# Two transformer blocks in one kernel on one core: order of work at the end of the second block's projections and at the start of its attention

## What is computed

```python
h = rms_norm(x, norm_g[l])
proj = h @ w_in[l]
cq, ckv, kr, dq, dk, dv, mq, z = jnp.split(proj, IN_OFFSETS_2, axis=-1)
y_mla  = mla_branch(cq, ckv, kr, ...)   # 8 heads; q from cq @ w_uq, k and v from ckv @ w_ukv, rms_norm per head, rope
y_diff = diff_branch(dq, dk, dv, ...)   # 4 heads with two maps each: p[0] - lam * p[1]
y_mem  = mem_branch(mq, mem, ...)       # 4 heads over 256 memory tokens
y = jnp.concatenate([y_mla, y_diff, y_mem], axis=-1) * jax.nn.silu(z)
x = x + y @ w_out[l]
```

## Time and profile before

| | |
|---|---|
| median of 3 runs | 1109.83 us (1109.31 to 1114.26) |
| the profiled execution | 1111.78 us, its span 1110.0 us |
| PE, busy | 1054.4 us (95%) |
| DVE, busy | 627.6 us (57%) |
| ACT, busy | 563.5 us (51%) |
| POOL, busy | 445.8 us (40%) |
| granted TensorE clock, mean | 0.982 |

### The profile page before, as it was taken

The page is one execution under the profiler, slowest core; times in us unless marked ns, Lnnn a source line. Parts: engine busy times, 40 slices in busy tenths (PEclk is TensorE's granted clock), DMA queues, the critical chain, the costliest instruction groups (busy, mean ns, idle before and its releaser), DMA issues.

```text
span 1110.0 us, 15249 instructions
## 1 busy us (share of the span) xinstructions
PE 1054.4 (95%) x5118; PEld 874.7 (79%) x5118; DVE 627.6 (57%) x1415; ACT 563.5 (51%) x1154; POOL 445.8 (40%) x215
## 2 busy tenths in 40 slices
PE   6999889999999999999999999999999989889798
PEld 4888778899888778888888888778887778666577
DVE  4536556888835466554545455442235988586732
ACT  5443667777724344444444444443244263887821
POOL 1444552343424443444444444414444244443323
PEclk9999999999999999999999999999999999898999
DMA  5364442111013332222223223243252122343213
GB/s 198 95 175 135 132 148 76 50 47 39 30 38 133 123 104 95 95 95 94 97 94 109 95 96 133 95 141 106 98 187 103 59 88 93 100 109 86 76 49 113
DMA packets 40604, 111.87 MB, mean 101 GB/s; under 512 B 7219, under 2 KB 10419, under 8 KB 39859
## 3 DMA queue, kind: packets, MB, share of 16 engines
q1 hardware_dynamic: 29724, 91.80, 25.3%
q10 hardware_dynamic: 10824, 19.35, 5.5%
HBM read 100.25 MB, written 7.96 MB: 97 GB/s over the span
## 4 chain that ended last, share of the span: by engine, by line
issue 44%; PE 26%; POOL 15%; DVE 8%; ACT 3%; DMA 1%; SPq 1%; POOLq 1%; ACTq 0%; DVEq 0%
POOL WLO L638 13%; PE PS L1816 6%; PE PS L1818 6%; PE PS L1817 6%; PE PS L1998 2%; PE PS L2021 2%; PE PS L1957 1%; PE PS L1958 1%; DVE PB L1326 1%; DMA X<-xT 1%; PE PS L2160 1%; ACT PB L879 1%; DVE BLO L1239 1%; DVE PB L1364 1%; ACT WHI L696 1%
## 5 line engine op out<-in xcount | busy, mean ns | idle before, releaser
L638 POOL TENSOR_TENSOR WLO<-RAW,WHI 128x1024 fp32r<-128x1024 f32 x155 | 376.4, 2429 | 542.7 <-ACT WHI L696 542.5
L696 ACT ACTIVATE WHI<-RAW 128x1024 fp32r<-128x1024 f32 x162 | 171.2, 1058 | 291.6 <-PE PS L1818 260.2
L1816 PE MATMUL PS<-HHI,WHI 128*128 128x512 f32 x648 | 257.4, 397 | 12.7 <-DVE HLO L1217 9.0
L1817 PE MATMUL PS<-HLO,WHI 128*128 128x512 f32 x648 | 255.0, 394 | 0.0
L1818 PE MATMUL PS<-HHI,WLO 128*128 128x512 f32 x648 | 254.6, 393 | 0.0
L1816 PEld LDWEIGHTS PS<-HHI,WHI 128*128 128x128 f32 x648 | 123.4, 190 | 41.1 <-issue 11.5
L1816 PE MATMUL PS<-BHI,WHI 128*128 128x512 f32 x368 | 145.2, 395 | 3.2 <-POOL WLO L638 1.8
L1818 PEld LDWEIGHTS PS<-HHI,WLO 128*128 128x128 f32 x648 | 123.4, 190 | 26.3
L1818 PE MATMUL PS<-BHI,WLO 128*128 128x512 f32 x368 | 143.4, 390 | 0.0
L1817 PE MATMUL PS<-BLO,WHI 128*128 128x512 f32 x368 | 143.3, 389 | 0.0
L1817 PEld LDWEIGHTS PS<-HLO,WHI 128*128 128x128 f32 x648 | 123.3, 190 | 25.3 <-issue 0.5
(11 more groups left out here) (316 smaller groups left out, 1675.7 us busy)
## 6 DMA issues: line engine op xcount, KB each, us to landing
RAW<-wstream SPq DMA_DIRECT2D x162, 512.0 KB, 3.2
X<-xT ACTq DMA_DIRECT2D x4, 512.0 KB, 9.5
bias_b<-bias_rows ACTq DMA_DIRECT2D x2, 1024.0 KB
FX<-bias_b ACTq DMA_DIRECT2D x8, 256.0 KB, 2.8
X<-xT ACTq DMA_DIRECT2D x8, 256.0 KB, 3.7
x_keep<-X ACTq DMA_DIRECT2D x2, 1024.0 KB, 6.0
X<-x_keep ACTq DMA_DIRECT2D x2, 1024.0 KB, 5.1
outT<-X ACTq DMA_DIRECT2D x8, 256.0 KB, 2.5
```

Source lines behind the costliest of these rows:

```text
L638: pool.tensor_tensor(WLO[:, s, :], RAW[:, s, :], WHI[:, s, :].bitcast(F), ALU.subtract).then_inc(split_lo, 1)
L696: act.activation(WHI[:, c % 2, :], RAW[:, c % 2, :], ACT.Copy).then_inc(split_hi, 1)
L1816: pe.matmul(dst, a[0], b[0], start=first, stop=False, **kw)
L1817: pe.matmul(dst, a[0], b[1], start=False, stop=False, **kw)
```

## The change

Weight units, places and heads:

```diff
-TAIL_UNITS = "c0 c1 c2 c3 d0 d1 d2 u4 d3 m0 m1 u5 m2 m3 uk6 z7 z0 z1 z2 uk7 z4 z3 z6 z5 ukv".split()
+TAIL_UNITS = "c0 c1 c2 c3 d0 d1 d2 u4 d3 m0 m1 m2 u5 m3 z7 z0 uk6 z1 z2 uk7 z4 z3 z6 z5 ukv".split()
-        STACK = [[lo(24), lo(25), lo(26), lo(27)], [lo(28), lo(29), lo(30), lo(31)],
-                 [lo(10), lo(11), lo(23), hi(31)], [lo(14), lo(15), hi(17), lo(17)]]
+        STACK = [[lo(10), lo(11), lo(23), lo(15)], [lo(24), lo(25), lo(26), lo(27)],
+                 [lo(28), lo(29), lo(30), lo(31)], [lo(14), hi(31), hi(17), lo(17)]]
-            plain([(256, 4, 64)], ..., [MQ, MQ + 1], v=(0, 256, DV), gain=[MQ_GAIN, MQ_GAIN]),
+            plain([(256, 4, 64)], ..., [MQ, MQ + 1], tb=4, v=(0, 256, DV), gain=[MQ_GAIN, MQ_GAIN]),
...
+            + [X[:, 4:8, :].rearrange("p a b -> p (a b)")]
```

SP: the first differential head is stacked between weight loads, 8 DMAs behind z4's load and 8 behind z3's; `stack_heads` begins with head 1; in `pair_heads` a wait stands ahead of the 16 DMAs of the memory heads' keys:

```diff
+                if c in (tail("z4"), tail("z3")):
+                    sp.wait_ge(h_lo, 4)
+                    sp.wait_ge(unit_used, tail("u5") + 1)
+                    stack_part(0, (tail("z4"), tail("z3")).index(c))
...
-                for h in range(4):
+                for h in range(1, 4):
...
+                sp.wait_ge(ATT["late"]["scores"], dm[5]["g1"])
```

POOL, and ACT inside the attention (i == -1 is behind the exponentials of map 0, i == 1 behind those of map 2) and in the tail:

```diff
-            low_halves(UNIT["down2"] + 1, UNIT["wout2"] + 2)
+            low_halves(UNIT["down2"] + 1, UNIT["wout2"])
             for m in LATE:
+                if m["i"] == 2:
+                    low_halves(UNIT["wout2"], UNIT["wout2"] + 2)
...
+                        if name == "late" and i == -1:
+                            act.wait_ge(lam_sum, 1)
+                            act.activation(LAM[:, 2:4], LAM[:, 0:2], ACT.Exp).then_inc(lam_exp, 1)
+                            used(tail("ukv"))
+                            for tk in range(NT):
+                                act.activation(whole(LV[tk]), PS[:, (4, 5, 6, 7)[tk], :], ACT.Copy).then_inc(vm_hi, 1)
+                        if name == "late" and i == 1:
+                            stream(UNIT["wout2"])
+                            stream(UNIT["wout2"] + 1)
...
             used(tail("u4"))
             mla_squares(2)
-            stream(UNIT["tail"] + 10)
             head_root(2)
             used(tail("d3"))
             head_evac(3)
+            stream(UNIT["tail"] + 10)
             head_square(3)
+            stream(UNIT["tail"] + 11)
             head_root(3)
             head_hi(2)
-            stream(UNIT["tail"] + 11)
             stream(UNIT["tail"] + 12)
+            stream(UNIT["tail"] + 13)
             used(tail("u5"))
             mla_squares(4)
-            stream(UNIT["tail"] + 13)
-            head_root(4)
             stream(UNIT["tail"] + 14)
...
             used(tail("m3"))
             head_evac(5)
+            stream(UNIT["tail"] + 15)
+            head_root(4)
+            head_square(5)
+            stream(UNIT["tail"] + 16)
             head_hi(3)
-            stream(UNIT["tail"] + 16)
-            head_square(5)
-            head_root(5)
-            head_hi(4)
             stream(UNIT["tail"] + 17)
             used(tail("uk6"))
             mla_squares(6)
+            head_root(5)
+            head_hi(4)
             stream(UNIT["tail"] + 18)
             head_root(6)
             stream(UNIT["tail"] + 19)
```

VectorE: the sums for lam move from behind `head_turned(3)` to ahead of `head_lo(7)`, their last two steps into the attention; `z_scale` 7 stands ahead of `head_norm(5)`, 0 ahead of `mla_norm(6)`, 1 behind it (bank 0 for 6); and the first map is biased ahead of z5:

```diff
             head_lo(7)
-            z_scale(5, 0)
...
             dve.wait_ge(h_tr, 8)
+            biased(ATT["late"], LATE[0])
+            z_scale(5, 3)
             attention("late")
```

TensorE:

```diff
             unit_tok(tail("m1"), ...)
-            pe.wait_ge(h_lo, 2)
+            unit_tok(tail("m2"), ...)
             pe.wait_ge(h_lo, 3)
             unit_tok(tail("u5"), 384, range(4), cq, 4, True, True)
-            unit_tok(tail("m2"), ...)
             unit_tok(tail("m3"), ...)
+            pe.wait_ge(*tok_at(5, 1))
+            unit_T(tail("z7"), 0, H).then_inc(unit_used, 1)
             pe.wait_ge(*tok_at(4, 4))
             head_turn(3)
             pe.wait_ge(*tok_at(5, 4))
+            unit_T(tail("z0"), 1, H).then_inc(unit_used, 1)
             pe.wait_ge(h_lo, 2)
             key_part(6, "uk6")
-            pe.wait_ge(*tok_at(5, 1))
-            unit_T(tail("z7"), 0, H).then_inc(unit_used, 1)
             head_turn(4)
-            pe.wait_ge(*tok_at(5, 2))
-            unit_T(tail("z0"), 1, H).then_inc(unit_used, 1)
-            pe.wait_ge(h_lo, 5)
-            unit_T(tail("z1"), 6, H).then_inc(unit_used, 1)
+            pe.wait_ge(scaled, SCALED["z"] + 1)
+            unit_T(tail("z1"), 0, H).then_inc(unit_used, 1)
             head_turn(5)
...
             head_turn(7)
+            A = ATT["late"]
             pe.wait_ge(scaled, SCALED["z"] + 6)
-            unit_T(tail("z5"), 0, H).then_inc(unit_used, 1)
+            pe.wait_ge(h_lo, 7)
+            scores(A, LATE[0])
+            pe.wait_ge(scaled, SCALED["z"] + 7)
+            unit_T(tail("z5"), 3, H).then_inc(unit_used, 1)
             pe.wait_ge(h_lo, 8)
             value_part()
+            scores(A, LATE[1])
             pe.wait_ge(scaled, SCALED["z"] + 8)
             attention("late")
```

More of the change, by code:

```diff
@@ L574, in _, with stack_part @@
             stream_pairs((UNIT["down2"] + 1) // 2, UNIT["tail"] // 2, 4)
+            def stack_part(h, m):
+                f = 64 * (h % 2) + 32 * m
+                rows = slice(f, f + 32)
+                for at in range(4):
+                    to = slice(32 * at, 32 * at + 32)
+                    sp.dma_start(STACK[h][2 * m][to, :].bitcast(F), part(at % 2, DQ + h // 2)[rows, :].bitcast(F)).then_inc(stacked[h], 16)
+                    sp.dma_start(STACK[h][2 * m + 1][to, :].bitcast(F), part(at // 2, DK + h // 2)[rows, :].bitcast(F)).then_inc(stacked[h], 16)
             def stack_heads():
-                sp.wait_ge(h_lo, 4)
                 sp.wait_ge(unit_used, UNIT["wout2"] - 1)
-                for h in range(4):
+                for h in range(1, 4):
                     if h == 3:
@@ L584, in stack_heads @@
                     for m in range(2):
[L585 to L590, removed]
+                        stack_part(h, m)
             def pair_heads():
@@ L598, in pair_heads @@
                     for w in range(2):
-                        to = slice(64 * w, 64 * w + 64)
-                        sp.dma_start(lo(24 + h)[to, :].bitcast(F), part(w, MQ + h // 2)[rows, :].bitcast(F)).then_inc(paired[h], 16)
+                        sp.dma_start(lo(24 + h)[64 * w:64 * w + 64, :].bitcast(F), part(w, MQ + h // 2)[rows, :].bitcast(F)).then_inc(paired[h], 16)
+                sp.wait_ge(ATT["late"]["scores"], dm[5]["g1"])
+                for h in range(4):
+                    rows = slice(64 * (h % 2), 64 * (h % 2) + 64)
+                    for w in range(2):
                         for half in (slice(0, 64), slice(64, 128)):
@@ L1109, in _, with silu @@
             stream(UNIT["tail"] + 9)
+            def silu(names):
+                for z in names:
+                    act.wait_ge(scaled, SCALED["z"] + 1 + ZS.index(z))
+                    n = int(z[1])
+                    act.activation(FX[:, n, :], FX[:, n, :], ACT.Silu).then_inc(z_done, 1)
             used(tail("u4"))
             mla_squares(2)
-            stream(UNIT["tail"] + 10)
             head_root(2)
@@ L1149, in _ @@
             head_root(7)
+            silu(ZS[0:4])
             stream(UNIT["tail"] + 22)
             stream(UNIT["tail"] + 23)
+            silu(ZS[4:6])
             stream(UNIT["tail"] + 24)
             head_hi(7)
[L1154 to L1161, removed]
+            silu(ZS[6:8])
             attention("late")
@@ L1374, in attention @@
                     steps = [(biased, i + 1), (normed, i)]
+                    if name == "late" and i == 1:
+                        dve.wait_ge(lam_exp, 1)
+                        link(dve.tensor_tensor(LAM[:, 0:1], LAM[:, 3:4], LAM[:, 2:3], ALU.subtract))
+                        link(dve.tensor_scalar(LAM[:, 0:1], LAM[:, 0:1], -LAM_INIT, None, ALU.add))
                     for f, j in steps:
-                        if 0 <= j < len(maps):
+                        if 0 <= j < len(maps) and (name == "ab" or f is normed or j > 0):
                             f(A, maps[j])
@@ L2034, in attention @@
                 A = ATT[name]
-                for i in range(-2, len(maps) + 2):
+                for i in range(0 if name == "late" else -2, len(maps) + 2):
                     if name == "late" and i == 0:
```

34 lines of the change are left out of this document (12 added, 22 removed).

## The result

| kernel | runs | median us | ratio to the kernel before, 95% interval |
|---|---|---|---|
| before | 20 | 1110.98 (1108.33 to 1115.48) | 1 |
| changed | 20 | 1113.82 (1111.94 to 1117.44) | 1.0027 (1.0016 to 1.0037) |
| changed, again | 12 | 1114.74 | 1.0030 (1.0012 to 1.0048) |
| before, again (`ctl`) | 12 | 1111.10 | 0.9996 (0.9977 to 1.0014) |

The change costs about 3 us: 2.8 in the first comparison, 3.7 in the second. The forecast was 1111.3 us, 1.5 us above the median then known, within 0.5%, and 1102 to 1117 us for the range.

What follows compares the result with a forecast made beforehand. VectorE, held up by collisions with POOL, was taken to set the start of head 6. Terms -2.9 (VectorE), +1.6 (clock) and +2.8 (late stage) sum to +1.5 us: median 1111.3 us, range 1102 to 1117.

Steps and rivals of the forecast that it cites:

- VectorE's chain to head 6 (U to H): From POOL's subtraction for d3 (U) to TensorE's transposes of head 6 (H): 2.9 us gained.
- low clock behind TensorE's idle piece (H to T): Head 6's transposes (H) to the end of head 7's (T): idle time slows the clock, +1.6 us, bounds 0 and 1.6.
- map 2 multiplied, from T: From the end of head 7's transposes: POOL's multiplication of map 2 ends at T+31.4, before at T+28.7.
- late stage to the end: Behind head 7's transposes: 2.8 us lost at map 2's multiplication and carried to the end, bounds -2.8 and +2.8.
- the middle taken for the collisions: VectorE ahead of head 6: 14.9 us of collisions with POOL, between 12.5 as before and 17.3 laid out.
- The layout: New order laid out piece by piece up to head 6: VectorE meets POOL's subtractions more often, 17.3 us of collisions.
- the work itself: VectorE from its scaling of head 2 to that of z2, without collisions: 49.9 us before, 49.4 after.
- The late stage: Scores of map 2 2.8 us sooner, but POOL's output projection halves delay its multiplication: 2.8 us behind.
- Early stacking at nothing: SP's queue: stacking the first differential head early, between weight loads, delays no load and costs nothing.
- TensorE alone could gain 11 us: Up to head 6's transposes: shorter waits and no slow clock would give TensorE 11 us, but VectorE forbids it.
- The 12.5 us of collisions before: Kernel before, VectorE ahead of head 6: eight places held up by POOL, 12.5 us together.
- Rival (2): Slower: more POOL collisions with VectorE, 857 to 922 us and in the maps, plus slow clocks: +7.3, 1117.1 us; 19%.

Runs made afterwards that it cites:

- again: The changed kernel once more, nothing edited: median 1114.74 us, ratio to the kernel before 1.0030.
- split11: Changed kernel with the output projection's weight halves later, ACT's behind the exponentials of map 10, POOL's ahead of its multiplication of map 11: 1111.76 us, ratio to before 1.0007.
- unstack: Changed kernel with the first differential head stacked with the others again, after z5 is used: 1120.84 us, ratio to before 1.0082.
- old_guard: Kernel before, with POOL's subtraction for z4 (and z3 behind it) waiting for VectorE's rotation of head 6: 1111.95 us, ratio 1.0002.
- endhalf: Changed kernel with POOL's two output projection subtractions behind its last multiplication of the late maps, ACT's halves left in place: 1112.05 us, ratio to before 1.0012.
- thin: Changed kernel with POOL's subtractions for units m1 to z3 on 64 of 1024 columns, rest not computed: 1107.00 us, ratio to before 0.9959.
- thin_old: Kernel before with POOL's subtractions for m1 to z3 on 64 of 1024 columns, rest not computed: 1106.92 us, ratio 0.9957.
- guard2: Changed kernel with endhalf's late stage, and POOL's subtractions for z4 and z3 waiting for VectorE's rotation of head 6: 1107.83 us, ratio to before 0.9967.

## Why the prediction was right or wrong

The side and the range were right: +1.5 us forecast, +2.8 and +3.7 measured, within 0.5%. The size was about half of what came, and even that owes something to luck: two terms are off, by 2.7 and 1.5 us, one each way. From the table of anchors:

| step | forecast | measured |
|---|---|---|
| VectorE's chain to head 6 (U to H) | -2.9, ends -5.3 and +0.8 | -0.2 (`again`, `split11`, `unstack`), -2.4 (first profile) |
| low clock behind TensorE's idle piece (H to T) | +1.6 | +1.4 to +2.2 |
| map 2 multiplied, from T | +2.7 | +1.8 |
| late stage to the end | +2.8, carried whole | 164.0 and 165.0, against 165.2, 162.0 and 162.5 (`old_guard`): +1.3 between the means, where profiles of one kernel lie up to 3.2 apart |

- **The bound was read rightly.** VectorE sets head 6, TensorE's gains end in one idle piece, and its clock is low behind it. The piece is longer than the 2 to 6 us of the forecast, 6.3 and 8.4, since TensorE comes sooner than was thought and, in `again`, VectorE later.
- **The step that failed is the middle taken for the collisions.** The layout gave 17.3 us, the prediction took 14.9 because each meeting hangs on tenths of a us. It did hang on 0.3 us, but it comes out the same way in four of five profiles with this order: `again` has 17.5, the first profile 15.3. The layout should have been taken as it stood. That is 2.6 of the 2.7 us by which this term was too fast; the work itself, 50.1 for 49.4 us, and the waits, smaller than forecast, nearly cancel.
- **The late stage** was right in mechanism: scores of map 2 at T+14.8, halves directly ahead of the multiplication, 2.8 us of idle ahead of map 3. `split11` and `endhalf` show the hold. Its size was 1 us too large at M (the sum takes 2.8 there, its own working gives 31.4 - 28.7 = 2.7, and 1.8 came). The carry to the end was too large too: in `split11` and `endhalf` 5.4 us were gained at M and 3 to 4 kept, though each met something new on the way. This error and that of the collisions are of opposite sign, and so the sum lies nearer than its terms.
- **Early stacking at nothing**: right, shown by `unstack`.
- **"TensorE alone could gain 11 us"**, 1.0 of them its wait ahead of head 6, was not tested as it stands. In both profiles of the changed kernel TensorE is ready for the transposes of head 6 at U+70.7, against U+78.2 before: 7.5 us sooner. In `thin` it is ready at U+67.9, some 10 us sooner, near the forecast; but `thin_old` is ready at U+71.7 with nothing but the collisions gone, and of the nearly 4 us between the two only 0.6 reach H.
- **The 12.5 us of collisions before** are 12.1, but taking each for time on the path overstated their worth: without them H comes 7.6 to 7.8 us sooner.
- **Rival (2)** had the collisions right (17 us), and its low clock behind map 2's hold came too, 979 to 989 us in `again` (table by stretch of TensorE, below); what it had too large is the late stage, +4.9 for +1.3. By the rule of the Trainium skill (SBUF — State Buffer, Who interferes with whom) an instruction of VectorE with two SBUF inputs contends with one of GpSimd that reads SBUF, and the one that comes second waits. The runs agree: 2.59 for 0.42 us, 2.32 for 0.16, each beside a subtraction that began first. The same section says that with at most one SBUF input, outside the two-port modes, there is no contention; L1672, L1740 and L1688 in `guard2` agree. Weighing the layout by that rule would have kept its 17.3 us.

```profile
979.00:990.00 11.00, 9.11 (x28) 0.53 0.37 91
```

## What to carry to other kernels

When VectorE is the full engine, ask of each GpSimd instruction beside it which VectorE instruction it meets. In `guard2`, starting GpSimd where VectorE reads PSUM or reduces cost nothing on the path; two such waits brought 4 us, and with the late halves moved a change that lost 3 us became a kernel 0.33% faster than the one before. The sum of all collisions is not their price: 17.5 us taken away brought 8.1, and VectorE waited for ACT in their place. And compare profiles by distances from an anchor ahead of the change, in more than one profile: here one pair of profiles lay 3.1 us apart before the change began, and two of the changed kernel 2.2 us apart at one collision.

## What the runs showed of the hardware

- POOL is held too: subtractions that met VectorE took 2.86 and 3.10 us in `again` (877.58 and 883.23 us) in place of 2.40. Of two subtractions in a row, each held VectorE once (`split11`, 1002.79 and 1005.14 us): VectorE got in between them.
- The same program meets the low clock at different lengths. TensorE alone, `ctl` and the first profile before, the same two maps:

```profile
998.00:1003.00 5.00, 4.71 (x15) 0.66 0.58 134
```

```profile
997.00:1004.00 7.00, 6.33 (x19) 0.52 0.49 113
```

From T to POOL's start on map 11 it is 66.0 us in the one and 68.3 in the other: 2.3 us, as much as most steps of this change.
